# Starting the expert stage of one token tile while the mixer of the other is still at work

## The reference, cut to what matters

```
h = h + merged @ w_mix_out                      # the mixer's last product
x = rmsnorm(h, ffn_norm_w)
q = (x @ w_query).reshape(b, s, HEADS, 2, 128)
s1, s2 = q[..., 0, :] @ keys_1.T, q[..., 1, :] @ keys_2.T
v1, i1 = top_k(s1, 16); v2, i2 = top_k(s2, 16)
top_score, pos = top_k(all 256 sums v1 + v2, 16)        # routing
experts = i1 * 128 + i2 at pos; gates = softmax(top_score)
act = gelu(x . expert_down[experts])            # dot products
y = sum over heads and k of gates * act * expert_up[experts]
out = rmsnorm(h + y, final_norm_w)
```

## Time and profile before

| | |
|---|---|
| median of 3 runs | 1478.37 us (1476.29 to 1478.59) |
| the profiled execution | 1479.0 us, its span 1477.2 us |
| busy: PE, DVE, ACT, POOL | 1316.6, 866.1, 473.5, 658.3 us |
| gathers | 36864 packets, 268.45 MB on queue q0 |
| chain that ended last, by engine | PE 59%, DMA 24%, DVE 9% |

### The profile page before, as it was taken

The page is one execution under the profiler, slowest core; times in us unless marked ns, Lnnn a source line. Parts: engine busy times, 40 slices in busy tenths (PEclk is TensorE's granted clock), DMA queues, the critical chain, the costliest instruction groups (busy, mean ns, idle before and its releaser), DMA issues.

```text
span 1477.2 us, 17718 instructions
## 1 busy us (share of the span) xinstructions
PE 1316.6 (89%) x6502; PEld 954.3 (65%) x6502; DVE 866.1 (59%) x1711; ACT 473.5 (32%) x815; POOL 658.3 (45%) x392
## 2 busy tenths in 40 slices
PE   5999998999989999999997889888778997787786
PEld 5997987998879999999875444344333443333332
DVE  3333243899236956432627585776677767677654
ACT  3564524443344424122101222232322232222211
POOL 5443246888846613320204345444344445444430
PEclk9999999999989999999998999999899999999998
DMA  7724243455443442314307899999999999999993
GB/s 273 287 82 169 109 159 115 177 195 199 177 165 115 171 170 88 112 61 143 115 1 305 327 397 410 421 421 423 420 421 422 421 421 422 421 421 421 421 421 141
DMA packets 53917, 389.92 MB, mean 264 GB/s; under 512 B 5176, under 2 KB 13512, under 8 KB 14152
## 3 DMA queue, kind: packets, MB, share of 16 engines
q0 software_dynamic: 36864, 268.45, 43.9%
q1 hardware_dynamic: 14432, 116.40, 21.2%
q10 hardware_dynamic: 2536, 3.95, 0.8%
HBM read 387.70 MB, written 1.07 MB: 263 GB/s over the span
## 4 chain that ended last, share of the span: by engine, by line
PE 59%; DMA 24%; DVE 9%; POOL 2%; issue 2%; ACT 1%; DVEq 0%; ACTq 0%; POOLq 0%
PE psum L500 58%; DMA work<-experts_dram,work 11%; DMA weight_ring<-experts_dram,work 10%; DVE work L1666 3%; DMA constants<-experts_dram,work 2%; POOL weight_lo L2134 1%; PE psum L630 1%; ACT work L2066 0%; POOL norm_stats L2124 0%; POOL work L2218 0%; DMA bias_rows_dram<-work 0%; DVE residual L1160 0%; DVE work L1653 0%; DVE work L1474 0%; DVE work L1655 0%
## 5 line engine op out<-in xcount | busy, mean ns | idle before, releaser
L500 PE MATMUL psum<-work 128*128 128x128 f32 (+6 forms) x1880 | 456.9, 400 | 68.7 <-ACT work L2066 66.2
L500 PEld LDWEIGHTS psum<-work 128*128 128x128 f32 (+2 forms) x1880 | 268.5, 194 | 244.5 <-issue 150.9
L2134 POOL TENSOR_TENSOR weight_lo<-weight_ring,weight_hi 128x2048 fp32r<-128x2048 f32 x64 | 299.4, 4679 | 183.7 <-ACT weight_hi L1736 159.9
L2218 POOL DMA_INDIRECT work<-experts_dram,work x153 | 177.1, 1158 | 242.6 <-PE psum L500 210.2
L1666 DVE CUSTOM_DVE_ANT_0 work<-work 128x1024 f32<-128x1024 f32 x153 | 187.6, 1226 | 98.7 <-DMA work<-experts_dram,work 86.9
L500 PE MATMUL psum<-weight_ring,work 128*128 128x512 f32 (+1 forms) x448 | 199.5, 590 | 40.1 <-ACT work L2066 37.8
L500 PEld LDWEIGHTS psum<-weight_ring,work 128*128 128x128 f32 (+1 forms) x448 | 81.2, 185 | 147.1 <-issue 85.9
L500 PE MATMUL psum<-normed_T,weight_ring 128*128 128x256 f32 (+1 forms) x768 | 159.2, 367 | 2.5 <-DVE work L1587 1.7
L1736 ACT ACTIVATE weight_hi<-weight_ring 128x2048 fp32r<-128x2048 f32 x66 | 125.8, 1913 | 88.6 <-PE psum L500 48.3
L500 PEld LDWEIGHTS psum<-normed_T,weight_ring 128*128 128x128 f32 x768 | 138.3, 195 | 23.9 <-issue 7.1
L500 PE MATMUL psum<-mlp_in_hi,weight_hi 128*128 128x256 f32 x504 | 145.3, 288 | 5.9 <-POOL weight_lo L2134 5.5
(11 more groups left out here) (261 smaller groups left out, 1708.6 us busy)
## 6 DMA issues: line engine op xcount, KB each, us to landing
weight_ring<-weights_dram SPq DMA_DIRECT2D x50, 2048.0 KB, 7.9
work<-weights_dram SPq DMA_DIRECT2D x3, 1024.0 KB, 6.3
work<-experts_dram,work POOLq DMA_INDIRECT x153, 31.2
weight_ring<-weights_dram SPq DMA_DIRECT2D x2, 1024.0 KB, 13.2
gain_rows<-gains_dram SPq DMA_DIRECT2D x2, 1024.0 KB, 10.3
work<-bias_rows_dram ACTq DMA_DIRECT2D x2, 1024.0 KB, 10.3
weight_ring<-experts_dram,work POOLq DMA_INDIRECT x80, 18.5
constants<-constants_dram ACTq DMA_DIRECT2D x1, 1094.0 KB, 9.4
```

Source lines behind the costliest of these rows:

```text
L500: return nc.tensor.matmul(o, l, r, start=start, stop=stop)
L2134: G_.tensor_tensor(low, loaded, high.bitcast(F32), ALU.subtract).then_inc(S("weight_lo_ready"), 1)
L2218: G_.indirect_dma_start(out=slots[s], out_offset=None, in_=experts, in_offset=bass.IndirectOffsetOnAxis(ap=expert[:, n % UNIT_BUFS, i:i + ...
```

## The change

- The order of routing (`FIRST_ROUTES`): unit 1's eight stages follow the dots 0 to 7 of unit 0, unit 2's follow dots 13 to 15 of unit 0 and 0 to 4 of unit 1, unit 3's lie in unit 1 from dot 5 on. Nothing stands between routing of unit 0 and the first dot but the four `add_dn` of tile 1.
- Unit 0's first coefficients come behind dot 4; `add_mixer` of tile 1 comes behind dots 4 and 6 (before: 1 and 3).
- On PE group 0 comes before tile 1's transposes and queries, group 1 before the key product of unit 2, group 2 before that of unit 3. ACT follows: the squares of tile 1 behind group 0's diagonals, its drains in groups 1 and 2, the exponentials of units 1 and 2 in groups 1 and 5.
- Banks of tile 1's dn_up are held out of the rotation until mix_out of tile 1 has begun.
- The delta-rule output is normed per tile; pooling's products 0 and 1 with the gates go before the norm, 2 and 3 behind the gating of tile 0.

```diff
@@ -429,9 +429,12 @@
     QUERY_DRAINS = {5: (1, 0), 6: (1, 1), 16: (2, 0), 20: (2, 1), 32: (3, 0), 36: (3, 1)}
     SCORE_DRAINS = {7: 1, 22: 2, 38: 3}
 
-    def route_after(n):
-
-        return (10, 11, 12, 13, 14, 14, 15, 15) if n == 0 else (3, 5, 7, 9, 11, 13, 14, 15)
+    FIRST_ROUTES = {(1, j): (0, j) for j in range(8)} | {(2, j): (0, 13 + j) if j < 3 else (1, j - 3) for j in range(8)} \
+        | {(3, j): (1, (5, 6, 8, 9, 11, 12, 14, 15)[j]) for j in range(8)}
+
+    def route_after(n, stage):
+
+        return FIRST_ROUTES[n, stage] if n < 4 else (n - 2, (3, 5, 7, 9, 11, 13, 14, 15)[stage])
 
     def slot_loaded(eng, m):
 
@@ -961,8 +964,8 @@
                     inner_parts()
             drained(pe, "pool", 1)
             up_proj("pool_up", pool_T, 4, {1: inner_parts})
-            pe.wait_ge(S("o_normed_ready"), 1)
             for t in range(TT):
+                pe.wait_ge(S("o_normed_ready"), t + 1)
                 for i in range(2):
                     ps = open_bank("dn_T", 2 * t + i)
                     for a in range(4):
@@ -973,6 +976,8 @@
 
                 pe.wait_ge(S(f"dn_up{j}_loaded"), 16)
                 ps = psum[:, filled["dn_up", 4 * t + j][0], :] if parts[0] else open_bank("dn_up", 4 * t + j)
+                if t and not parts[0]:
+                    held_banks.append(filled["dn_up", 4 * t + j][0])
                 for a in parts:
                     for k in range(KC):
                         if j == a == 0 and k % 4 == 0:
@@ -1058,12 +1063,11 @@
             first_queries(1)
             mix_out(0, 1, (0, 1))
             first_key_products(1)
+            held_banks.clear()
             mix_out(0, 1, range(2, KC))
             slab_read("mix_out", 1)
             mix_out(1, 1)
             slab_read("mix_out", 3)
-            expert_in_T(1)
-            first_queries(2)
             for t in range(TT):
                 for half in range(2):
                     open_bank("y", 2 * t + half)
@@ -1088,9 +1092,13 @@
                     up_group(n, k)
                     G = group_number(n, k)
                     if G == 0:
+                        expert_in_T(1)
+                        first_queries(2)
+                    if G == 1:
                         first_key_products(2)
                         first_queries(3)
                         slab_read("query0", 3)
+                    if G == 2:
                         first_key_products(3)
                     if G in QUERY_QUARTERS:
                         s, quarters = QUERY_QUARTERS[G]
@@ -1556,20 +1564,26 @@
             settle(V.tensor_tensor(stat[:, 0, 5, :], stat[:, 0, 5, :], q_norm2.rearrange("p t h -> p (t h)"), ALU.mult))
             V.tensor_scalar(stat[:, 1, 5, :], stat[:, 0, 5, :], 1.0 / P, EPS, ALU.mult, ALU.add).then_inc(S("variance_ready"), 1)
             landed(dve, "variance_ready")
+            def gate_pooled(i):
+
+                ps = full(dve, "pool_up", i).rearrange("p (a n) -> p a n", a=2)
+                free(V.tensor_tensor(mixed2_T[:, 2 * i:2 * i + 2, :], ps, gate_a2[:, 2 * i:2 * i + 2, :], ALU.mult), "pool_up", i)
+
+            drained(dve, "gate2_a0", 1)
+            drained(dve, "gate2_a1", 1)
+            for i in range(2):
+                gate_pooled(i)
             rstd_done(dve, 5)
             settle(V.tensor_tensor(stat[:, 2, 5, :], stat[:, 2, 5, :], kq_norms[:, 1, :, :].rearrange("p t h -> p (t h)"), ALU.mult))
-            V.tensor_tensor(o_tok[:, :, :], o_tok[:, :, :], bc(stat[:, 2, 5, :], [P, UNITS, P], 2), ALU.mult)\
-                .then_inc(S("o_normed_ready"), 1)
-            landed(dve, "o_normed_ready")
-            for i in range(4):
-                if i == 0:
-                    drained(dve, "gate2_a0", 1)
-                    drained(dve, "gate2_a1", 1)
-                ps = full(dve, "pool_up", i).rearrange("p (a n) -> p a n", a=2)
-                free(V.tensor_tensor(mixed2_T[:, 2 * i:2 * i + 2, :], ps, gate_a2[:, 2 * i:2 * i + 2, :], ALU.mult), "pool_up", i)
+            for t in range(TT):
+                u = slice(t * HEADS, (t + 1) * HEADS)
+                V.tensor_tensor(o_tok[:, u, :], o_tok[:, u, :], bc(stat[:, 2, 5, u], [P, HEADS, P], 2), ALU.mult).then_inc(S("o_normed_ready"), 1)
+                landed(dve, "o_normed_ready")
             drained(dve, "z0", 1)
             drained(dve, "z1", 1)
-            for t in range(TT):
+
+            def gate_outputs(t):
+
                 for i in range(2):
                     ps = full(dve, "dn_T", 2 * t + i).rearrange("p (a c n) -> p a c n", a=4, c=2)
                     z = z_T[:, 4 * i:4 * i + 4, t * P:(t + 1) * P].rearrange("p a (c n) -> p a c n", c=2)
@@ -1577,6 +1591,11 @@
                         last = V.scalar_tensor_tensor(out=z[:, :, c, :], in0=ps[:, :, 1 - c, :], scalar=PR("dn_norm"), in1=z[:, :, c, :],
                                                       op0=ALU.mult, op1=ALU.mult)
                     free(last, "dn_T", 2 * t + i)
+
+            gate_outputs(0)
+            for i in range(2, 4):
+                gate_pooled(i)
+            gate_outputs(1)
             drained(dve, "gate2_b0", 1)
             drained(dve, "gate2_b1", 1)
 
@@ -1698,21 +1717,23 @@
                 route(0, stage)
             for j in range(4):
                 add_dn(j, 1)
-            for stage in range(8):
-                route(1, stage)
             for n in range(UNITS):
                 for i in range(TOPK):
                     dot(n, i)
-                    if n == 0 and i in (1, 3):
-                        add_mixer(1, i // 2)
-                    for stage in range(8):
-                        if n + 2 < UNITS and i == route_after(n)[stage]:
-                            route(n + 2, stage)
+                    if n == 0 and i == 4:
+                        gates(0)
+                        coefs(0, 0)
+                    if n == 0 and i in (4, 6):
+                        add_mixer(1, i // 2 - 2)
+                    for later in range(n + 1, min(n + 3, UNITS)):
+                        for stage in range(8):
+                            if route_after(later, stage) == (n, i):
+                                route(later, stage)
                     if n and i == 0:
                         coefs(n - 1, 3)
-                    if i == 4:
+                    if i == 4 and n:
                         gates(n)
-                    if i in (4, 8, 12):
+                    if i in (4, 8, 12) and (n or i > 4):
                         coefs(n, i // 4 - 1)
                     if n == UNITS - 2 and i == 9:
                         dve.wait_ge(S("dots_done"), n * TOPK + i + 1)
@@ -2074,20 +2095,25 @@
                 drain_first_query(n)
                 drain_first_scores(n)
             gate_exp(0)
-            gate_exp(1)
-            mixer_squares(1, 0)
-            mixer_squares(1, 1)
-            drain_expert_in(1)
-            drain_first_query(2)
             for n in range(UNITS):
                 for k in range(len(groups(n))):
+                    G = group_number(n, k)
                     gelu(n, k)
+                    if G == 1:
+                        drain_expert_in(1)
                     diagonals(n, k)
-                    G = group_number(n, k)
                     if G == 0:
+                        mixer_squares(1, 0)
+                        mixer_squares(1, 1)
+                    if G == 1:
+                        drain_first_query(2)
+                        gate_exp(1)
                         drain_first_scores(2)
+                    if G == 2:
                         drain_first_query(3)
                         drain_first_scores(3)
+                    if G == 5:
+                        gate_exp(2)
                     if G in QUERY_DRAINS:
                         drain_query(*QUERY_DRAINS[G])
                     if G in SCORE_DRAINS:
@@ -2096,7 +2122,7 @@
                             act.wait_ge(S("routed"), 4 * (s - 1))
                         for t in range(TT):
                             drain_scores(s, t)
-                if n + 2 < UNITS:
+                if 1 <= n < UNITS - 2:
                     gate_exp(n + 2)
```

## The result

The changed kernel takes 1466.52 us (median of 5 runs, 1464.12 to 1469.00) against 1478.37 (median of 5, 1475.69 to 1479.76): 11.9 us less, ratio 0.9925 with a 95% interval of 0.9908 to 0.9942. The forecast was 1468.4, its range 1466 to 1473. The profiled execution takes 1466.5 us instead of 1479.0, its span 1464.7 instead of 1477.2.

A forecast was written before the change was run, and what follows sets the result against it. The prediction took DMA transfers of a fixed amount of bytes behind a start as the bound. Gains of 1.95 + 7.0 + 1.05 = 10.0 us take the profiled 1479.0 to 1469.0, as a median 1468.4 us, range 1466 to 1473.

The forecast's parts named there:

- The bound: Expert stage: a fixed amount of bytes, its end set by the first gather's issue and later DMA idling or slowness.
- Norm part: Ahead of dn_up: PE's wait for DVE's gating goes and the first gather moves with it, 1.95 us (bounds 0 and 2.1).
- Held banks: Queries of unit 1: their 1.71 us wait for DVE goes, worth nothing in the sum, making room for group 0.
- Idle stretch: DMA engines almost still from 818 to 825 us before gather 13: goes away with group 0 early, 7.0 us.
- The stretch to 900 us: DMA from 825 to 900 us: most of a 1.5 us loss goes as PE leads by more, 1.05 us (bounds 0 and 1.5).
- The sum: Whole kernel: 1.95 + 7.0 + 1.05 = 10.0 us gained.
- slow ramp: DMA engines after the idle stretch: a microsecond, with the spread of runs, added to the largest gain, giving 1466.
- The first: Rival at the start: dn_up stays at 733.4 and the first gather does not move, 1470.4 us; chance 0.08.
- The second: Rival in groups 1 or 2: ACT's in-order waits bring 4 us of idle DMA behind gather 16, 1472.4 us; chance 0.08.
- The third: Rival in unit 0: PE stays at the lower clock throughout, 13.7 us lost, 1482 us, slower than before; chance 0.04.

The follow-up runs named there:

- Act_free: The changed kernel with the scalar engine's copies of the key products of units 2 and 3 one group later: 1465.98 us.
- old_routes: The changed kernel with the routing of units 2 and 3 where it was before the change: 1466.05 us.
- norm_only: The kernel before with only the norm per tile and two pooling products ahead of it: 1474.02 us, ratio 0.9974 to the kernel before.
- no_hold: The changed kernel without the banks of tile 1's dn_up held out of the rotation: 1466.82 us.
- slots10: The changed kernel with 10 instead of 13 row slots until row 171: 1469.79 us.
- slots runs: The changed kernel with 11, 10, 9 or 8 instead of 13 row slots until row 171: 1467.70, 1469.79, 1489.65 and 1548.9 us.
- early_only: The changed kernel with the old norm put back, one for both tiles with four pooling products behind it: 1469.62 us.
- early_again: The same kernel as early_only, the changed kernel with the old norm, measured in another series: 1470.79 us.

## Why the prediction was right, and the terms that were too small

- *The bound.* A fixed amount of bytes behind a start was right. Act_free removed a wait of 7 us on DVE, old_routes moved one, and neither changed the time; fewer slots changed the rate of transfer and cost up to 82 us.
- *Norm part, 1.95 us.* The mechanism was right, the term too small, and the bound of 2.1 too low. From the end of the pooling product to the first gather it took 53.61 us before and 51.10 after, 2.5 us less: the wait of 1.94, 0.20 ahead of the transposes, and the rest by instructions that now overlap. The profiled execution of the change was 0.67 us late ahead of that, so the raw 1.84 looks like my figure by chance. In the medians the part is worth 3 to 4 us. Of the 5.4 us of norm_only's profile, 1.7 are the clock of PE's last records, which this part of the change does not touch, and 1.5 lie between the first gather and the last landings. The lower clock behind the wait of 1.94 us can be a part too: it cost 1.6 us in two of the three profiles of kernels with that wait, but the one profile of the kernel before does not show it. What the medians gain above 2.5 us stays open.
- *Held banks, nothing.* Right, by no_hold.
- *Idle stretch, 7.0 us.* Right: group 0 at 800.3 (forecast 800.6), gather 13 at 809.0 (810), gather 17 at 818.95 (819). In bytes it was 6.8 us.
- *The stretch to 900 us, 1.05 us.* This is the mis-sized term. I read the loss from the share, 0.99 against 1.01; by the rate it is 75 us x (421 - 396) / 421 = 4.5 us, beyond my bound of 1.5, and all of it went. The kernel before came out of its idle stretch with empty queues and stood at 9 us from issue to landing in 865 to 890; in the changed one no landing that the trace times in 825 to 900 takes less than 15.5. Whether the lost rate came from the short queue or from PE, which freed too few slots, is not separated.
- *The sum.* The parts by the profile are 1.84 + 6.8 + 4.5 = 13.1 us of lead at 900 us, and 12.5 at the last landing and at the end. The 0.6 between was not traced; the rates are rounded to 1 GB/s, and half of that over 540 us is 0.6 us. The forecast was 10.0 and its bounds added up to 10.6, less than the 11.9 measured. That 1466.52 lies inside the range, half a microsecond from its end, is owed to the microsecond added for the slow ramp and the spread of runs, and in part to luck.
- *The rivals.* The first, an unmoved start, fell: the first gather went out 1.84 us earlier. The second, a new wait that gives time back, fell: the waits came and cost nothing that shows. The third, PE at the lower clock throughout, fell: the clock was 1.00 from 800 to 810, and only the queries of unit 2, behind a wait of 3.02 us, took 5.43 instead of 3.74 us.

## What to carry to other kernels

Where a stage is bound by transfers, ask for the first issue, and then for GB/s and the time from issue to landing in every stretch. As long as the rate stays full, a wait on a compute engine costs nothing, as those of 7 us did here. When landings come within some 10 us of the issue, bytes can be lost although the engines read as busy, so take the loss from GB/s and not from the share. The stall that emptied the queue cost twice here: 6.8 us while it lasted and 4.5 us in the stretch behind it. Before a gain of 2 us is read from two profiles, compare them ahead of the changed part and in the tail: here they differed there by up to 2.9 and 1.7 us.

## What was not expected of the hardware

The rate of gathers of 8 KB rows against the median time from issue to landing was 419 to 422 GB/s at 10.3 us and above in six windows of slots10 between 840 and 1100 us, and 420 at 9.8 (norm_only, 840 to 865). It was 405 at 9.4 (slots10, 960 to 1000), 394 at 9.0 (norm_only, 865 to 890) and 382 at 9.2 (the kernel before, 865 to 890). The share was 0.98 to 1.02 in all of them. The exceptions stand with the slots runs.

A drop of the granted clock does not follow from the length of a wait alone. For dn_up behind 1.94 us the clock fell in two profiles and not in a third. For the 16 records of group 0 it fell behind 2.32 us (no_hold, 8.80 us, clock 0.50 from 802 to 804) and behind 3.19 us (act_free, 8.64 us), and did not behind 3.48 us (the changed kernel) and 3.29 us (early_only), 7.11 us in both. For the twelve records at the end it fell behind 2.87 us (before) and 2.41 us (changed), 7.11 us in both, and did not behind 3.25 us (early_again), 5.42 us.
